# The second MLP's junction: x times the norm weights made ahead, x itself updated behind the low parts

## What is computed

```python
def rmsnorm(x, g):
    xf = x.astype(jnp.float32)
    y = xf * lax.rsqrt(jnp.mean(xf * xf, axis=-1, keepdims=True) + EPS)
    return (y * g.astype(jnp.float32)).astype(x.dtype)

    # second block, layer i
        m = diff_attention(h, ...)                     # ends with o @ w_o
        x = x + rmsnorm(m, norm_mixer_post[i])
        h = rmsnorm(x, norm_mlp_pre[i])
        x = x + rmsnorm(sq_relu_mlp(h, mlp_w_up[i], mlp_w_down[i]), norm_mlp_post[i])
```

## Time and profile before

| | us |
|---|---|
| median of 3 runs | 1962.97 |
| lowest and highest | 1962.93, 1963.45 |
| the profiled execution, whole | 1962.8 |
| its span in the profile | 1961.0 |
| TensorE busy in the span | 1940.6 |
| VectorE busy | 1262.1 |
| ScalarE busy | 849.3 |
| GpSimd busy | 133.0 |

### The profile page before, as it was taken

The page is one execution under the profiler, slowest core; times in us unless marked ns, Lnnn a source line. Parts: engine busy times, 40 slices in busy tenths (PEclk is TensorE's granted clock), DMA queues, the critical chain, the costliest instruction groups (busy, mean ns, idle before and its releaser), DMA issues.

```text
span 1961.0 us, 22627 instructions
## 1 busy us (share of the span) xinstructions
PE 1940.6 (99%) x9791; PEld 1642.1 (84%) x9791; DVE 1262.1 (64%) x1081; ACT 849.3 (43%) x876; POOL 133.0 (7%) x188
## 2 busy tenths in 40 slices
PE   9999999999999999999999999999999999999998
PEld 8788888888988888898888888888898889888886
DVE  8465587755485866477776695866464466775835
ACT  5454463352353453344555453453242235453432
POOL 0100142010100000030000100000020010000000
PEclk9999999999999999999999999999999999999999
DMA  5222122223323223143221413323323333323221
GB/s 194 95 65 82 69 65 78 74 86 118 129 86 129 94 78 108 65 127 91 72 70 66 150 65 129 108 65 108 108 71 106 107 107 119 129 68 126 85 87 65
DMA packets 99106, 188.44 MB, mean 96 GB/s; under 512 B 4398, under 2 KB 16832, under 8 KB 99008
## 3 DMA queue, kind: packets, MB, share of 16 engines
q1 hardware_dynamic: 94704, 176.17, 26.8%
q0 software_dynamic: 4016, 10.77, 1.9%
q10 hardware_dynamic: 288, 0.07, 0.0%
HBM read 183.85 MB, written 2.10 MB: 95 GB/s over the span
## 4 chain that ended last, share of the span: by engine, by line
PE 91%; DVE 5%; ACT 2%; POOL 1%; issue 1%; DMA 0%; DVEq 0%; POOLq 0%; ACTq 0%
PE ps L891 30%; PE ps L1053 18%; PE ps L1162 11%; PE ps L1038 8%; PE ps L855 5%; PE ps L915 5%; PE ps L1413 2%; PE ps L1407 2%; PE ps L1360 1%; PE ps L949 1%; PE ps L1266 1%; PE ps L1432 1%; DVE w_lo L2171 1%; PE ps L1218 1%; PE ps L1190 1%
## 5 line engine op out<-in xcount | busy, mean ns | idle before, releaser
L2171 DVE TENSOR_TENSOR w_lo<-w_raw,w_hi 128x2048 fp32r<-128x2048 f32 x153 | 354.6, 2318 | 345.4 <-ACT w_hi L1614 344.5
L1614 ACT ACTIVATE w_hi<-w_raw 128x2048 fp32r<-128x2048 f32 x153 | 293.0, 1915 | 537.3 <-PE ps L891 329.9
L891 PE MATMUL ps<-a_hi,w_hi 128*128 128x512 f32 x640 | 249.0, 389 | 0.0
L891 PE MATMUL ps<-a_lo,w_hi 128*128 128x512 f32 x640 | 249.0, 389 | 0.0
L891 PE MATMUL ps<-a_hi,w_lo 128*128 128x512 f32 x640 | 249.0, 389 | 0.0
L1053 PE MATMUL ps<-w_hi,h_hi 128*128 128x512 f32 x504 | 197.0, 391 | 1.2 <-issue 1.2
L1053 PE MATMUL ps<-w_hi,h_lo 128*128 128x512 f32 x504 | 196.3, 389 | 0.0
L1053 PE MATMUL ps<-w_lo,h_hi 128*128 128x512 f32 x504 | 196.1, 389 | 0.0
L891 PEld LDWEIGHTS ps<-a_hi,w_lo 128*128 128x128 f32 x640 | 120.1, 188 | 25.1
L891 PEld LDWEIGHTS ps<-a_lo,w_hi 128*128 128x128 f32 x640 | 120.1, 188 | 24.8
L891 PEld LDWEIGHTS ps<-a_hi,w_hi 128*128 128x128 f32 x640 | 120.1, 188 | 24.7
(11 more groups left out here) (429 smaller groups left out, 3896.8 us busy)
## 6 DMA issues: line engine op xcount, KB each, us to landing
w_raw<-in_mlp_w_up SPq DMA_DIRECT2D x32, 1024.0 KB, 5.4
w_raw<-in_w_ff SPq DMA_DIRECT2D x26, 1024.0 KB, 5.3
w_raw<-in_w_in SPq DMA_DIRECT2D x24, 1024.0 KB, 5.1
w_raw<-in_mlp_w_down SPq DMA_DIRECT2D x20, 1024.0 KB, 5.0
w_raw<-in_attn_w_qkv SPq DMA_DIRECT2D x12, 1024.0 KB, 5.2
arena<-in_mlp_w_down SPq DMA_DIRECT2D x12, 1024.0 KB, 7.4
w_raw<-in_conv_w_in SPq DMA_DIRECT2D x12, 1024.0 KB, 5.0
arena<-in_w_ff SPq DMA_DIRECT2D x6, 1024.0 KB, 7.9
```

The source lines that it names most:

```text
L891: last = mm(ps[:, bank0 + j], left, right, start=(k == 0 and x == 0), stop=(k == QUAD * quads - 1 and x == 2), skip_group_check=halves)
L1614: nc.scalar.activation(w_hi[:, n % 2], raw_at[raw_slot[n]], ACT.Copy).then_inc(hi_ready, 1)
L2171: tt(w_lo[:, n % 2], raw_at[raw_slot[n]], w_hi[:, n % 2].bitcast(F32), ALU.subtract).then_inc(lo_ready, 1)
```

## The change

- GpSimd fetches two rows ahead, into tmp: g_pre = norm_mlp_pre and g_both = norm_mixer_post. VectorE multiplies g_both by g_pre, and makes x_gained(i) = x_tm(i) x g_pre for the four tiles, in h_hi's place. These five operations stand in the list of attention's last two heads.
- In the junction, gained, summed and weighted are replaced by turn_gained (y_gained = y_tm x g_both) and turn_summed (y_gained = y_gained x r + x_gained, raising normed). TensorE turns y_gained in place of y_tm.
- The order on VectorE is new, and early stands ahead of turn_summed(1). Behind low(3) come four pairs that update x: y_tm = y_tm x g_add, then, after a wait for this, x_tm = y_tm x r + x_tm, raising resid_ready.
- GpSimd fetches g_add once, where it did, and no g_turn there; it waits for resid_ready of all four tiles, where it waited for normed, ahead of the rows of the next junction. The counts of grow_in in the later junctions go up by one.
- TensorE's and ScalarE's orders are unchanged. The other junctions keep theirs.

The diff, without the branches that lose their cases for this junction and without the counts:

```diff
+        x_gained = h_hi_f.rearrange("p (a b) -> p a b", a=TT)
+        g_pre, g_both = tmp[:, 0:D], tmp[:, D:2 * D]
...
+            pool.wait_ge(rope_done, 2 * PAIRS)
+            gain_row(g_pre, "norm_mlp_pre_2", 0)
+            gain_row(g_both, "norm_mixer_post_2", 0)
+            pool.wait_ge(grow_in, 80)
             pool.wait_ge(quad_done, first_part + 2)
             pool.wait_ge(o_mm, DIFF_HEADS)
             gain_row(g_add, "norm_mixer_post_2", 0)
-            gain_row(g_turn, "norm_mlp_pre_2", 0)
             refine_tiles("h_mlp1")
-            pool.wait_ge(normed, 12)
+            pool.wait_ge(resid_ready, 4 * junctions["h_mlp1"][3] + TT)
             gain_row(g_add, "norm_mlp_post_2", 0)
...
-                                                   y_tm[:, i, P * k:P * (k + 1)], ident)
+                                                   (y_gained if name == "h_mlp1" else y_tm)[:, i, P * k:P * (k + 1)], ident)
...
+                def turn_gained(i):
+                    dve.wait_ge(*((tile_out, tile0 + i + 1) if i < TT - 1 else (banks_free, after_block[name])))
+                    tt(y_gained[:, i], y_tm[:, i], g_both, ALU.mult).then_inc(y_ready, 1)
+
+                def turn_summed(i):
+                    dve.wait_ge(rstd_ready, root_count(name, add, i))
+                    dve.wait_ge(y_ready, first_y + i + 1)
+                    stt(y_gained[:, i], y_gained[:, i], rstd[add % 2][:, i:i + 1], x_gained[:, i],
+                        ALU.mult, ALU.add).then_inc(normed, 1)
+
+                if name == "h_mlp1":
+                    moved(0)
+                    turn_gained(0)
+                    moved(1)
+                    turn_gained(1)
+                    turn_summed(0)
+                    early()
+                    turn_summed(1)
+                    moved(2)
+                    low(name, 0)
+                    low(name, 1)
+                    moved(3)
+                    mid_split()
+                    turn_gained(2)
+                    turn_summed(2)
+                    last_split()
+                    turn_gained(3)
+                    turn_summed(3)
+                    low(name, 2)
+                    low(name, 3)
+                    dve.wait_ge(grow_in, 16 * rows)
+                    for i in range(TT):
+                        step(tt(y_tm[:, i], y_tm[:, i], g_add, ALU.mult))
+                        stt(x_tm[:, i], y_tm[:, i], rstd[add % 2][:, i:i + 1], x_tm[:, i], ALU.mult, ALU.add).then_inc(resid_ready, 1)
+                    return
                 if name in unscaled:
...
             o_sums(6)
+            dve.wait_ge(grow_in, 80)
+            step(tt(g_both, g_both, g_pre, ALU.mult))
+
+            def x_gain(i):
+                tt(x_gained[:, i], x_tm[:, i], g_pre, ALU.mult)
+
             diff_mix(7)
             o_norm(6)
+            x_gain(0)
             diff_low(7)
             split_quad(first_part + 3)
             o_low(6, 5)
+            x_gain(1)
             o_sums(7)
             o_norm(7)
+            x_gain(2)
             o_low(7, DIFF_OUT)
+            step(tt(x_gained[:, 3], x_tm[:, 3], g_pre, ALU.mult))
             dve.wait_ge(part_out, 6)
```

More of the change, by code:

```diff
@@ L2468, in junction @@
                     moved(1)
-                    if name != "h_mlp1":
-                        gained(1)
+                    gained(1)
                     summed(0)
                     weighted(0)
-                    if name == "h_mlp1":
-                        gained(1)
                     summed(1)
@@ L2477, in junction @@
                     early()
[L2478 to L2493, removed]
+                    mid_split()
+                    moved(2)
+                    low(name, 0)
+                    gained(2)
+                    low(name, 1)
+                    moved(3)
+                    gained(3)
                     summed(2)
                     weighted(2)
-                    if name == "h_mlp1":
-                        gained(3)
                     last_split()
@@ L3056, in add_first @@
                 tt(d, ps[:, 2:4], d, ALU.add).then_inc(banks_free, 1)
-            junction("h_mlp1", add_parts, 5, lambda: split(ph["w_o"], 0, 0, 0), held_split("w_o", 0), add_first)
+            junction("h_mlp1", add_parts, 6, lambda: split(ph["w_o"], 0, 0, 0), held_split("w_o", 0), add_first)
             mlp("mlp1", 4 + MLP_CHUNKS, 4 + MLP_F32, y_tm)
-            junction("h_conv", add_tile("mlp1", y_tm), 7, held_split("mlp1", 0), held_split("mlp1", 1))
+            junction("h_conv", add_tile("mlp1", y_tm), 8, held_split("mlp1", 0), held_split("mlp1", 1))
             def conv(k):
@@ L3106, in _ @@
             body(ph["conv_out"], 0, 0, to_tokens(y_tm))
-            junction("h_mlp2", move_tile("conv_out", y_tm), 9, held_split("conv_out", 0), held_split("conv_out", 1))
+            junction("h_mlp2", move_tile("conv_out", y_tm), 10, held_split("conv_out", 0), held_split("conv_out", 1))
             mlp("mlp2", 4 + 2 * MLP_CHUNKS + 8, 4 + 2 * MLP_F32 + 8, y_tm)
-            junction("out", add_tile("mlp2", y_tm), 10, lambda: None, lambda: None)
+            junction("out", add_tile("mlp2", y_tm), 11, lambda: None, lambda: None)
 _OUT = ((1, SEQ, D), "float32")
```

## The result

| | before | after |
|---|---|---|
| median of 15 runs, us | 1963.22 | 1967.65 |
| lowest and highest | 1962.73, 1963.79 | 1966.75, 1968.72 |
| the profiled execution | 1962.8 | 1968.25 |
| its span | 1961.0 | 1966.5 |
| granted TensorE clock, mean (1 is 2.4 GHz) | 0.999 | 0.997 |

A forecast was written before the change was run, and what follows sets the result against it. TensorE's own time, 91% of the chain, bounds the kernel. Savings of 0.47, 0.33 and 1.40 us up to turn 3 (-2.20), then a 4.5 us stall, lengthen the junction 2.48 us: 1962.97 + 2.5 = 1965.5 us, range 1963.2 to 1967.6.

The forecast's parts named there:

- the likeliest sum: The forecast as summed: whole junction 2.48 us longer, time 1965.5 us, its own range 1964.8 to 1966.1; chance 0.62.
- the second case: Rival: the 4.5 us stall sends TensorE to the slow rate, 1.7 to 1.9 us lost, 1967.3 us; chance 0.17.
- the third one: Rival: turn 3 stays as late as it was; 1967.2 us with only 0.47 recovered, 1967.7 with nothing; chance 0.08.
- Before the junction: Five added VectorE operations between 1059 and 1082 us each fit an idle gap; cost 0, bounds 0 and +0.3 us.
- Tiles 0 and 1: Turns stay behind the fillers; VectorE frees earlier, so TensorE's wait for the first a_lo shrinks by 0.47 us.
- Tiles 2 and 3: TensorE's wait for the second quad's w_lo goes, -0.33 us, and its wait for the last turned tile, -1.40 us.
- a late root: At turn 3, GpSimd's root waiting out one more product (+0.8 us) would be late by 0.1 us.
- The tail: Updates of x delay ScalarE's squares, then u2's w_hi and w_lo; TensorE's first u2 product at 1125.00, stall 4.5 us.
- One of the signs: In the profile after, VectorE would show no gap between 1083 and 1120 us.
- Behind that, nothing gives it back: After u2's late start, later MLP waits move with TensorE's products, so the 2.5 us is not recovered.
- The clock: Whether the 4.5 us stall behind u1's products brings back the slow rate, 0.41 against 0.24 us a product; chance 0.17.
- The bound: TensorE's four waits at 1082 to 1135 us give back at most 3.1 us, 0.16%; a 0.2% gain is out of reach.

The follow-up runs named there:

- the kernel with the squares behind: The changed kernel with ScalarE rounding u2's weights (w_hi) first and squaring the four tiles of x after that; 1962.69 us, ratio 0.9996.
- tail cut: The changed kernel with x's fourth update behind u2's w_lo, and ScalarE squaring tile 2 behind u2's w_hi, tile 3 behind u3's; 1961.08 us; without the eight fillers 1958.93.
- the fillers in the stall: The changed kernel with 18 products of the identity put on TensorE between u1's and u2's products; 1965.73 us, ratio 1.0012.
- the stall of 2.85 us: The kernel before, with five more squares on ScalarE behind the four of x, so u2's weights come late; 1967.76 us, ratio 1.0021.
- the stall of 5.03 us: The kernel before, with seven more squares on ScalarE behind the four of x; 1970.82 us, ratio 1.0038.

## Why the prediction was right, and where it was not

The direction was right, and so was the chain that makes the kernel slower. The size was not: the likeliest sum gives 2.5 us of the 4.4, and the time lies at the edge of the range only because the range was drawn to take in the second case as well. The time by itself could not have told the cases apart: the third one, with nothing recovered ahead of the tail, stood at 1967.7, as near to 1967.65 as anything, and only the trace excludes it.

- **Before the junction, 0.** Right. The five products lie in their gaps; the one ahead of o_sums(7) left 0.42 us. The junction begins 0.2 us later in the profile after (1082.35 against 1082.15), but the stretch at 1057.9, ahead of the first added product, is already 0.17 late, and in the kernel with the squares behind, which has the same head, the fillers start 0.06 us earlier than before.
- **Tiles 0 and 1, -0.47.** Right: from the first products of the MLP to those behind a_lo it is 1.45 us, it was 1.91. Turns 0 and 1 stood behind the fillers as said.
- **Tiles 2 and 3, -1.73.** Right, -1.8: up to turn 3 it is 2.28 us less in all, 2.20 was said. GpSimd's pow for tile 3 took 1.65 us, more than the 1.40 of the earlier trace rows, and was ready at 1102.2, 3 us ahead of turn_summed(3). So the 0.1 that the prediction's range kept for a late root was misread: it compared the root with TensorE's 0.7 us to spare, not with the time at which VectorE comes to it.
- **The tail.** Right in its chain and within 0.2 us at every step: fourth square 1119.44 (1119.64 said), w_hi 1120.50 (1120.70), first product of u2 1124.86 (1125.00), a stall of 4.33 us (4.5). A pair takes 2.45 us, not 2.52, because the stt follows its tt by 1.25 us. The two kernels that reorder ScalarE and VectorE show that it is this chain, and that ScalarE's queue has most of it. One of the signs was wrong: VectorE has gaps between 1083 and 1120 us, 2.46 ahead of the first a_lo and 0.64 ahead of the last two. Its own sum had the first: turn 1 ready at 1090.8, moved(2) behind it, and a_lo only at 1093.74. Neither gap costs anything.
- **Behind that, nothing gives it back.** Right: the delay only grows, 5.07 us at the MLP's first sum and 5.5 at the end.
- **The clock.** This is the step that failed. The prediction took the stall, 4.5 us, to leave the clock alone with a chance of 0.62 against 0.17. It gave the length of the stall, that it was three times the longest wait of the trace, and that the kernel's own first products run at half the pace. Against it stood only that TensorE had been busy for long, which did not help: in the executions with a trace, stalls of 2.85, 4.33 and 5.03 us all brought 0.50, the first and the last in the kernel before. The sign that it named came, products 0.43 us apart behind the stall. Its price for this case, 1.7 to 1.9 us, was near, where the medians show 2.1 and the profiled execution 2.7; in part that is luck, since the stretch that it was read from, the start of the kernel, varies by 1 us itself. The rule of the Trainium skill named there (TensorE: Matmul & The Clock Gate, What's actually happening) told the outcome; the granted clock of 0.50 behind the stall agrees with it. A forecast with the clock's price in its sum, 1965.5 + 1.8 = 1967.3, would have been 0.35 us off.
- **The bound.** The prediction called a gain of 0.2% out of reach, counting the waits of TensorE alone. For the change as it stands that holds; but the fillers are 1.8 us of work whose results nobody reads, and with them gone the same change, its tail cut, is 0.23% faster than before. They should have been counted with the waits.

## What to carry to other kernels

When work is moved off the path "behind" something, look who waits for its result and what stands behind that waiter in its engine's queue: here four squares that nobody needs for long held up weights that were needed at once. A new wait of TensorE of the lengths seen here, 2.85 us and more, has to be priced with the slow products behind it, here 1.7 to 2.7 us in the traces, on top of its length. And after a change has made an operand early, look again for work that was there to fill the wait for it.

## What the runs showed that was not expected

- Waits of 0.89, 0.34 and 1.50 us with products of 1.1 and 1.2 us between them were followed by a granted clock of 0.69 in the next 1.4 us (1096.8 to 1098.2) and 0.58 in the 3 us behind that. The single wait of 1.22 us in the kernel with the squares behind, and of 0.31 us behind the fillers in the stall, left it at 1.00.
- The kernel's start differs from execution to execution. TensorE's first four products of 128x512, in the kernel before and with the stall of 2.85 us:

```profile
5.17 1.17 PE L949 MATMUL ps<-h_hi,w_hi 128*128 128x512 f32 x4
```

```profile
5.33 2.05 PE L949 MATMUL ps<-h_hi,w_hi 128*128 128x512 f32 x4
```

  In the second the slow pace lasts longer, and VectorE is 1.04 us late at 50 us and still 0.9 late at 1050 us, ahead of the edit. It is the same with the stall of 5.03 us (1.97 us, and 0.98 late). Both profiled executions are slower than their medians, by 0.9 and 0.7. The fastest and the slowest run of one kernel lie 1.1 to 2.9 us apart in all kernels but one (0.8), and a slow stretch behind a stall does not decide it: 2.0 after and 1.3 with the stall of 5.03 us, but 1.9 with the tail cut, where the clock stays up. So a single run can't tell such kernels apart to better than 1 us. How much of the scatter comes from the start is not shown.
- In the first 4 us of the kernel, read as a stretch of its own, the granted clock is 1.00 although ten products take 4.09 us, and in the execution above the four products that take 2.05 us lie in a stretch (5 to 8 us) with 1.00 as well. Behind a stall the column reads 0.50 for products at half the pace. So either it is no witness for the start of a kernel, or the start is slow for another reason; no run here decides. The 40 slices that the prediction read it from are 49 us each, too long to show 4 us.
